# Token halves in block 1's feed-forward norm, and an early mean with squares per tile in block 2's norm

## The reference

```python
def first_block(...):                      # for l in range(2)
    ...
    x = x + g1 * (mix @ w_out[l])
    h = rmsnorm(x, norm_ffn_g[l]) * (1.0 + sc2) + sh2
    f = (silu(h @ ffn_w1[l]) * (h @ ffn_w3[l])) @ ffn_w2[l]
    x = x + g2 * f

def second_block(...):                     # for i in range(2)
    ...
    mix = concat([a_out, b_out]) @ w_o[i]
    x = layer_norm(ALPHA * x + mix, ln1_g[i], ln1_b[i])
    gate, up = split(x @ w_ffn_in[i], 2)
    ffn = (silu(gate) * up) @ w_ffn_out[i]
    ple = (p[i] @ w_ple[i]) * sigmoid(x @ w_ple_gate[i])
    x = layer_norm(ALPHA * x + ffn + ple, ln2_g[i], ln2_b[i])
```

## Time and profile before

| | before |
|---|---|
| median of 3 runs | 2498.53 us (2494.79 to 2498.84) |
| profiled execution | 2500.13 us |
| its span | 2498.3 us |
| mean granted clock of PE | 0.992 |
| busy: PE, DVE, ACT, POOL | 97%, 71%, 44%, 43% |

### The profile page before, as it was taken

The page is one execution under the profiler, slowest core; times in us unless marked ns, Lnnn a source line. Parts: engine busy times, 40 slices in busy tenths (PEclk is TensorE's granted clock), DMA queues, the critical chain, the costliest instruction groups (busy, mean ns, idle before and its releaser), DMA issues.

```text
span 2498.3 us, 35167 instructions
## 1 busy us (share of the span) xinstructions
PE 2424.8 (97%) x13615; PEld 2033.0 (81%) x13615; DVE 1765.1 (71%) x2671; ACT 1095.0 (44%) x1803; POOL 1065.5 (43%) x600
## 2 busy tenths in 40 slices
PE   6999999999999999999999999999999999999997
PEld 4777788988777788998777779999877777999985
...
DMA packets 239645, 268.87 MB, mean 108 GB/s; under 512 B 19976, under 2 KB 204024, under 8 KB 239224
## 3 DMA queue, kind: packets, MB, share of 16 engines
...
HBM read 264.51 MB, written 2.10 MB: 107 GB/s over the span
## 4 chain that ended last, share of the span: by engine, by line
PE 75%; DVE 10%; issue 5%; ACT 4%; POOL 3%; DMA 3%; SPq 1%; ACTq 0%; DVEq 0%; POOLq 0%
PE bank L2801 22%; PE bank L2803 22%; PE bank L2802 22%; DVE k_lo L2057 1%; DMA raw<-in_w_ffn_in 1%; DVE r L1908 1%; POOL w_lo L1652 1%; POOL k_lo L1663 1%; DMA raw<-in_ffn_w 1%; ACT k_hi L1105 1%; DVE u_sum L2074 1%; PE bank L3404 1%; PE bank L3470 1%; DVE u_t_raw L2087 1%; PE bank L3130 1%
## 5 line engine op out<-in xcount | busy, mean ns | idle before, releaser
L1663 POOL TENSOR_TENSOR k_lo<-raw,k_hi 128x512 fp32r<-128x512 f32 x297 | 430.0, 1459 | 542.9 <-ACT k_hi L1105 541.9
L1652 POOL TENSOR_TENSOR w_lo<-raw,w_hi 128x2048 fp32r<-128x2048 f32 x53 | 248.8, 4694 | 525.3 <-ACT w_hi L1051 446.3
L1105 ACT ACTIVATE k_hi<-raw 128x512 fp32r<-128x512 f32 x444 | 270.9, 626 | 310.7 <-PE bank L2803 249.4
L2801 PE MATMUL bank<-h_hi,k_lo 128*128 128x256 f32 (+1 forms) x1156 | 370.8, 321 | 3.8 <-DVE k_lo L2057 2.5
L2802 PE MATMUL bank<-h_lo,k_hi 128*128 128x256 f32 (+1 forms) x1156 | 369.6, 320 | 0.0
L2803 PE MATMUL bank<-h_hi,k_hi 128*128 128x256 f32 (+1 forms) x1156 | 369.5, 320 | 0.0
L2801 PE MATMUL bank<-h_hi,w_lo 128*128 128x512 f32 x800 | 325.0, 406 | 10.7 <-DVE h_lo L2017 3.9
L2803 PE MATMUL bank<-h_hi,w_hi 128*128 128x512 f32 x800 | 313.4, 392 | 0.0
L2802 PE MATMUL bank<-h_lo,w_hi 128*128 128x512 f32 x800 | 313.3, 392 | 0.0
L2801 PE MATMUL bank<-f_hi,k_lo 128*128 128x512 f32 x704 | 278.4, 395 | 8.6 <-DVE u_row L2118 2.9
L2801 PE MATMUL bank<-u_t_hi,k_lo 128*128 128x256 f32 x1008 | 282.6, 280 | 1.2 <-POOL k_lo L1663 1.2
...
## 6 DMA issues: line engine op xcount, KB each, us to landing
...
```

The source lines that it names most:

```text
L1105: act.activation(hi, src, ACT.Copy).then_inc(s.f_hi.up, 1)
L1652: pool.tensor_tensor(b.w_lo[p][:, 0:n], b.raw[p][:, 0:n], b.w_hi[p][:, 0:n].bitcast(F32), ALU.subtract)\
L1663: pool.tensor_tensor(lo, src, hi.bitcast(F32), ALU.subtract).then_inc(s.f_lo.up, 1)
L2801: pe.matmul(out, wlo, xhi, start=start, stop=False)
```

## The change

Block 1: the last tile of w_out is multiplied in two halves of 256 tokens, into two banks, behind `columns(1)`. Sum of squares, root, gain and shift and low part are done for the left 256 tokens and then for the right ones, with the sum for the left half inside the right half's products and that for the right half behind the first step of the feed-forward. `first_units` runs all eight channel tiles for the left half, then all for the right half, without dummies ahead of it; it counts `f_step` in the second half alone. The signals of the norm count halves, and SP waits for the right half's first low part before two loads of `b_raw`.

Block 2: while PE begins w_o, DVE sums the eight tiles of x as they are before w_o is added, PE makes the mean of this after the first k of `attended`, and DVE subtracts it. ACT squares each tile of x as w_o's tile is added (ahead of `split(15)`), PE sums four of the squares ahead of w_o's last tile and the others after it, with the mean of what the tiles now hold. The variance is the mean square less the square of this mean, and DVE subtracts the remaining mean tile by tile while it scales.

The core of the diff (the signals' counts, renamed signals and arguments that are only passed through are left out):

```diff
+HALVED = 1, 3
+LAST_BANK = 2, 1
...
-    sp.wait_ge(*s.hl(l * 2 + 1, 1))
+    sp.wait_ge(*s.hl(l * 2 + 1, KD + 1))
...
+def act_half_root(act, e, c, h):
+    s, b, bank, v = e.s, e.b, e.bank, HALVES[h]
+    act.wait_ge(*s.rms(c, 2 + h))
+    act.activation(b.r[:, v], bank[7][:, v], ACT.Ln, bias=b.eps[:, 0:1], scale=1.0 / D).then_inc(s.r.up, 1)
+    act.wait_ge(*s.r(c, 2 * h + 1))
+    act.activation(b.r[:, v], b.r[:, v], ACT.Exp, scale=-0.5).then_inc(s.r.up, 1)
+def act_half_scaled(act, e, c, h, gain, shift, full, ks):
+    s, b, v = e.s, e.b, HALVES[h]
+    for k in ks:
+        act.wait_ge(*s.xr(c, (KD + 1) * h + (k + 2 if k else 1)))
+        bias, scale = shift[:, k:k + 1], gain[:, k:k + 1]
+        act.activation(b.h_hi[:, k, v], b.sq[:, k, v], ACT.Identity, bias=bias, scale=scale).then_inc(s.hh.up, 1)
+        if k:
+            act.activation(full[:, k, v], b.sq[:, k, v], ACT.Identity, bias=bias, scale=scale).then_inc(s.hf.up, 1)
+def act_halves(act, e, c, gain, shift, full):
+    act_half_root(act, e, c, 0)
+    act_half_scaled(act, e, c, 0, gain, shift, full, range(0, 5))
+    act_half_root(act, e, c, 1)
+    act_half_scaled(act, e, c, 0, gain, shift, full, range(5, KD))
+    act_half_scaled(act, e, c, 1, gain, shift, full, range(KD))
...
         act_high(act, e, lay, q)
-    act_rms(act, e, l * 2 + 1, b.gain[:, 8:16], b.mod[:, 24:32], b.hf)
+    act_halves(act, e, l * 2 + 1, b.gain[:, 8:16], b.mod[:, 24:32], b.hf)
...
 def act_layer_norm(act, e, l):
     s, b, bank = e.s, e.b, e.bank
-    for k in range(KD):
-        act.wait_ge(*s.ld(l, k + 1))
-        act.activation(b.sq[:, k, :], b.x[:, k, :], ACT.Square).then_inc(s.lsq.up, 1)
     act.wait_ge(*s.lmean(l, 2))
-    act.activation(b.r[:, :], bank[7][:, :], ACT.Ln, bias=b.eps[:, 1:2], scale=1.0 / D).then_inc(s.l_r.up, 1)
-    act.wait_ge(*s.l_r(l, 1))
+    act.activation(b.sq[:, 1, :], bank[6][:, :], ACT.Square, scale=1.0 / D).then_inc(s.l_r.up, 1)
+    act.wait_ge(*s.var(l, 1))
+    act.activation(b.r[:, :], b.sq[:, 1, :], ACT.Ln, bias=b.eps[:, 1:2]).then_inc(s.l_r.up, 1)
+    act.wait_ge(*s.l_r(l, 2))
     act.activation(b.r[:, :], b.r[:, :], ACT.Exp, scale=-0.5).then_inc(s.l_r.up, 1)
     act_normed(act, e, l * 2, 0)
+def act_square_out(act, e, l, ks):
+    s, b = e.s, e.b
+    for k in ks:
+        act.wait_ge(*s.res(l, k + 1))
+        act.activation(b.sq[:, k, :], b.x[:, k, :], ACT.Square).then_inc(s.lsq.up, 1)
...
     split(14)
+    act_square_out(act, e, l, range(KD))
     split(15)
...
-    dve_square(dve, e, KD - 1, b.sq[:, KD - 1, :], lay.bank_out(1, Q_OUT + 1))
+    c, last = l * 2 + 1, KD - 1
     dve.wait_ge(*s.b_pe(l, 1))
     dve_gains(dve, e, l, 1)
+    def last_tile(h, signal):
+        v = HALVES[h]
+        dve.scalar_tensor_tensor(b.x[:, last, v], bank[LAST_BANK[h]][:, v], b.mod[:, 16 + last:17 + last],
+                                 b.x[:, last, v], ALU.mult, ALU.add).then_inc(signal.up, 1)
+    def last_square(h):
+        v = HALVES[h]
+        dve.tensor_tensor(b.sq[:, last, v], b.x[:, last, v], b.x[:, last, v], ALU.mult).then_inc(s.ssq.up, 1)
+    gain, shift = b.gain[:, 8:16], b.mod[:, 24:32]
+    dve.wait_ge(*s.rms(c, 1))
+    last_tile(0, s.ssq)
+    dve.wait_ge(*s.ssq(c, 7))
+    last_square(0)
+    dve.wait_ge(*s.tile(lay.pair(6), 1, 1))
+    last_tile(1, s.bank[1])
     dve.wait_ge(*s.gain(l, 2))
-    dve_rms(dve, e, l * 2 + 1, b.gain[:, 8:16], b.mod[:, 24:32], b.hf, s.hl)
+    dve_half_root(dve, e, c, 0, 0)
+    dve_half_full(dve, e, c, 0, gain, shift, b.hf)
+    dve_half_root(dve, e, c, 0, 1)
+    dve.wait_ge(*lay.bank_out(1, Q_OUT + 1))
+    last_square(1)
+    for k in range(2, KD):
+        dve_half_low(dve, e, c, 0, k - 2, b.hf, s.hl)
+        dve_half_root(dve, e, c, 0, k)
+    for k in (KD - 2, KD - 1):
+        dve_half_low(dve, e, c, 0, k, b.hf, s.hl)
+        dve_half_root(dve, e, c, 1, k - (KD - 2))
+        if k == KD - 2:
+            dve_half_full(dve, e, c, 1, gain, shift, b.hf)
+    for k in range(2, KD):
+        dve_half_low(dve, e, c, 1, k - 2, b.hf, s.hl)
+        dve_half_root(dve, e, c, 1, k)
+    for k in (KD - 2, KD - 1):
+        dve_half_low(dve, e, c, 1, k, b.hf, s.hl)
...
 def dve_layer_norm(dve, e, l):
     s, b, bank = e.s, e.b, e.bank
-    dve.wait_ge(*s.lmean(l, 1))
+    dve.wait_ge(*s.l_r(l, 1))
+    dve.wait_ge(*s.lmean(l, 3))
+    dve.scalar_tensor_tensor(b.sq[:, 1, :], bank[7][:, :], 1.0 / D, b.sq[:, 1, :], ALU.mult, ALU.subtract)\
+       .then_inc(s.var.up, 1)
+    for k in range(2):
+        dve_less_mean(dve, e, k, -1.0 / D)
+    dve.wait_ge(*s.l_r(l, 3))
     for k in range(KD):
-        dve.scalar_tensor_tensor(b.x[:, k, :], bank[6][:, :], -1.0 / D, b.x[:, k, :], ALU.mult, ALU.add)\
-           .then_inc(s.ld.up, 1)
-    dve.wait_ge(*s.l_r(l, 2))
-    for k in range(KD):
-        dve.wait_ge(*s.ld(l, k + 1))
+        dve.wait_ge(*s.ld(l, KD + k + 1))
         dve_scaled(dve, e, k)
         if k == 0:
             dve_normed(dve, e, l * 2, 0)
+        if k + 2 < KD:
+            dve_less_mean(dve, e, k + 2, -1.0 / D)
...
+def dve_early_shift(dve, e, lay, l):
+    s, b = e.s, e.b
+    for k in range(2):
+        dve.wait_ge(*lay.bank_out(k % 2, PART_USE[KD - 2 + k]))
+    dve.tensor_tensor(b.r[:, :], b.x[:, 0, :], b.x[:, 1, :], ALU.add).then_inc(s.lsum.up, 1)
+    for k in range(2, KD):
+        dve.wait_ge(*s.lsum(l, k - 1))
+        dve.tensor_tensor(b.r[:, :], b.r[:, :], b.x[:, k, :], ALU.add).then_inc(s.lsum.up, 1)
+    dve.wait_ge(*s.lmean(l, 1))
+    for k in range(KD):
+        dve_less_mean(dve, e, k, -1.0 / D)
...
+    dve_early_shift(dve, e, lay, l)
     for k in range(KD):
+        dve.wait_ge(*s.ld(l, k + 1))
         dve.wait_ge(*(s.att(l, 3 * (k // 4) + k % 4 + 1) if k % 4 < 3 else
                       s.tile(lay.pair(6), k // 4, 1)))
-        dve.wait_ge(*lay.bank_out(k % 2, PART_USE[k]))
         dve.tensor_tensor(b.x[:, k, :], b.x[:, k, :], bank[OUT2_BANK[k]][:, :], ALU.add).then_inc(s.res.up, 1)
...
+def pe_half_rms(pe, e, c, h, total, last):
+    s, v = e.s, HALVES[h]
+    pe.wait_ge(*s.ssq(c, 8 + h))
+    pe.matmul(e.bank[7][:, v], e.b.ones[:, :], total[:, v], start=True, stop=False)
+    pe.matmul(e.bank[7][:, v], e.b.ones[:, :], last[:, v], start=False, stop=True).then_inc(s.rms.up, 1)
+def pe_last_out(pe, e, lay, total):
+    s, b, c, j2, p = e.s, e.b, lay.l * 2 + 1, 6, 1
+    hi, lo = w8(b.w_hi[p]), w8(b.w_lo[p])
+    for h in range(2):
+        pe.wait_ge(*(lay.bank_free(1, Q_OUT + 1) if h else s.mo(lay.l, 1)))
+        v = HALVES[h]
+        for n, k in enumerate(MIX_ORDER):
+            if (h, n) == (1, 6):
+                pe_half_rms(pe, e, c, 0, total, b.sq[:, KD - 1, :])
+            op = three(pe, e.bank[LAST_BANK[h]][:, v], hi[:, k, P:2 * P], lo[:, k, P:2 * P], b.h_hi[:, k, v], b.h_lo[:, k, v],
+                       n == 0, n == KD - 1)
+        op.then_inc(s.half.up if h else s.rms.up, 1)
...
-        keep_busy(pe, e, bank[0])
-        for k in range(4):
-            for q in (k, 4 + k):
-                pe.wait_ge(*s.low_in(n, plan, q))
-            for c in range(2):
-                pe.wait_ge(*ready(2 * k + c))
-                for u in range(2):
-                    for m in range(2):
-                        op = plain(u, k, m, c, 2 * k + c, k == 0 and c == 0, k == 3 and c == 1)
-            op.then_inc(s.f_step.up, 1 if k < 3 else RING - 3)
+        for h in range(2):
+            for k in range(4):
+                if h == 0:
+                    for q in (k, 4 + k):
+                        pe.wait_ge(*s.low_in(n, plan, q))
+                for c in range(2):
+                    pe.wait_ge(*ready(h, 2 * k + c))
+                    for u in range(2):
+                        for m in range(2):
+                            op = plain(u, k, m, c, 2 * k + c, k == 0 and c == 0, k == 3 and c == 1, HALVES[h])
+                if h:
+                    op.then_inc(s.f_step.up, 1 if k < 3 else RING - 3)
+                elif k == 0:
+                    halfway(None, 0)
...
-    for j in range(2):
-        pe_unit(pe, e, lay, 12 + j, Q_OUT + j, order=MIX_ORDER)
+    pe_unit(pe, e, lay, 12, Q_OUT, order=MIX_ORDER)
+    pe_unit(pe, e, lay, 13, Q_OUT + 1, order=MIX_ORDER, ms=(0,))
     columns(1).then_inc(s.b_pe.up, 1)
-    pe_rms(pe, e, c + 1, b.sq[:, 0, :], b.sq[:, KD - 1, :])
-    pe_ffn(pe, e, lay, lambda k: s.hl(c + 1, k + 1), between)
+    pe_last_out(pe, e, lay, b.sq[:, 0, :])
+    def halfway(u, at):
+        pe_half_rms(pe, e, c + 1, 1, b.sq[:, 0, :], b.sq[:, KD - 1, :])
+    pe_ffn(pe, e, lay, lambda h, k: s.hl(c + 1, KD * h + k + 1), between, halfway)
...
 def pe_layer_norm(pe, e, l):
     s, b, bank = e.s, e.b, e.bank
-    pe.wait_ge(*s.lsum(l, 6))
+    pe_square_sums(pe, e, l, range(4, KD - 1))
+    pe.wait_ge(*s.lsum(l, 13))
+    pe.wait_ge(*s.ld(l, KD))
     pe.matmul(bank[6][:, :], b.ones[:, :], b.r[:, :], start=True, stop=False)
     pe.wait_ge(*s.res(l, KD))
```

(58 more changed lines are left out.)

40 lines of the change are left out of this document (22 added, 18 removed).

## The result

| | before | after |
|---|---|---|
| median | 2497.75 us (4 runs) | 2535.74 us (2531.98 to 2539.88, 4 runs) |
| profiled execution, its span | 2500.13, 2498.3 us | 2539.88, 2538.1 us |
| mean granted clock of PE | 0.992 | 0.983 |

The ratio is 1.0154, with a 95% interval of 1.0134 to 1.0175: 38 us slower, where 33.6 were forecast. In the profiled executions it is 39.75.

A forecast was written before the change was run, and what follows sets the result against it. TensorE, busy 97% of the span, was taken as the bound. Block 1's 5.2 and block 2's 11.6 us, over two layers, made 33.6 on 2500.13, 2533.7, less 1.6: 2532; range 2519 to 2542, with 0.8 between 2506 and 2542.

The forecast's parts named there:

- W_out's last tile, copies, root: Block 1, end of w_out: tile ends 1.9 us later, k_hi copies run 263.85 to 266.05, root there at 266.95.
- Restart of block 1: Block 1: VectorE's half operations wait for GpSimd's k_lo, first low part ends 271.4, TensorE restarts at 271.5: +1.0 us.
- The bound with nothing stalled: Block 1's restart if no VectorE operation waits for GpSimd: TensorE restarts at 268.85, -1.65 us.
- First units: Block 1's first units: 192 half-width matmuls plus the second half sum, 23.7 us for 21.90 (+1.8), plus 2 for half clock.
- rival E: Every extra matmul pays its weight load, 0.187 us, 240 of them, 45 us over the forecast: 2577 us, chance 0.02.
- The other side of block 1: Block 1, ScalarE's doubled scalings: 2.6 us more, TensorE's next unit +3.9 to +5.9; +5.2 a layer taken, bounds +2 and +6.5.
- rival C: Later waits in block 1's feed-forward swallow most of the 5.2 us, block 2 at its least +2.3: 2503 us, chance 0.08.
- SP's later b_raw loads: Block 1: two loads start some 10 us later, costed at nothing since their columns are wanted only after four feed-forward units.
- The early mean: Block 2, w_o: VectorE's seven adds, taking turns with GpSimd, stall TensorE 6.6 us a layer, plus 2 for the clock.
- Sums and restart of block 2: Block 2 after w_o: TensorE idles 3 us for GpSimd's w_lo before the dummies; first product +2.3 to +3.9, taken +3.
- Rival B: Block 2: adds are through before TensorE asks, no stall and no lost clock in w_o: 2517 us, chance 0.20.
- A: The forecast itself, 2532 us, chance 0.63; own range 2519 (block 1 at +2, block 2 at +9) to 2542.

The follow-up runs named there:

- the three edits: Changed kernel with 18 dummies ahead of block 1's first units, the second half's sum early and the left root ahead of ScalarE's k_hi copies: 2528.37 us, ratio 1.0123.

## Why the prediction was right

2535.74 lies in the range; the forecast of 2532 is 3.7 low. Block 2 came as worked out, and its room up to +15 a layer went unused; that kept the total in the range although block 1, 10.1 and 7.7 a layer, lies above its own bound of +6.5. So the nearness of the total is in part luck. Step by step:

- **W_out's last tile, copies, root: right.** Copies at 7.71 from the mark (forecast 7.65), root at 10.70 (10.75), POOL's k_lo at 8.41 (8.3).
- **Restart of block 1: right in kind, +0.45 for +1.0.** DVE's operations were held, two of them, not all. The half sum that comes early gives nothing, as forecast, but the run with the root ahead shows that ScalarE's queue, which the prediction blamed, isn't the only reason: GpSimd would have held VectorE anyway. (The bound with nothing stalled, 268.85, is 0.35 less than five operations of 0.45 from 266.95 give; the forecast doesn't use it.)
- **First units: right.** 26.1 us with the second sum and the half clock, 25.7 forecast. The 196 instructions in these 26.1 us, part of them at half clock, leave no room for a weight load paid by each: rival E is out. In the halved tile, whose matmuls each load 128 columns of weights, 39 matmuls start in 4.68 us, 0.12 each (the x41 counts two that began earlier), while the loads run beside them all that time. By the Trainium skill (TensorE: Matmul & The Clock Gate, "The mechanism") a load overlaps running matmuls only where their row groups differ; the trace doesn't agree with that sentence for this case, and the same section also lets a load into the background weight buffer go ahead.

```profile
256.34:261.02 4.68, 4.68 (x41) 4.68 (x40) 2.26 (x6) 0.48 (x1) 0.00 (x0) 1.00 0.00 0
```

- **The other side of block 1: mis-sized.** This is the step that failed: "ACT's 15 scalings of some 0.7 become 30 of 0.44, 2.6 more", and from it "+3.9 to +5.9". The next unit came 8.9 later. A half scaling has a pitch of 0.50 and not 0.44, so 30 take 14.9, where 15 whole ones take 10.6 (0.708 a step from 270.95 to 280.16 in the run with the whole norm): 4.3 more. And I missed that ScalarE's second root stands behind the scalings of the left half's first five tiles, and waits 2.83 for a sum that PE makes behind 24 matmuls, nearly all at half clock. The wait of 4.69 that this gives PE drew a second stretch of half clock. Making the norm whole again took 15.0 of 18.6 away, which shows that the halves of the norm, not the halved tile, are the cost. How the last scaling's 9.3 divide is read from ScalarE's rows: 4.3 for the operations, and 6.1 for gaps between the scalings (6.5 where they were 0.5: 2.2 behind the first scaling, for a DVE operation held beside GpSimd; 3.8 for the second sum and root; 0.6 for DVE), less 1.1 for the sooner start. Of this the three edits show 3.2.
- **Later waits took part of it back.** PE's 0.93 at 315.17 and, in the second layer, 2.36 at 960.01 of the kernel before have no counterpart after; the waits of 2.88 and 2.26 remained, at 3.10 and 2.27. So rival C's mechanism was there, at small size. SP's later b_raw loads, put at nothing, end no wait of PE over 0.25 us in the first layer.
- **The early mean: right.** 5.62 and 5.64 of wait for 6.6; the adds took the turns that were worked out, from 1425.54 to 1440.98 (15.4, forecast 16.0). Both runs on this term, POOL held back and the mean asked for later, behave by their marks as the mechanism says.
- **Sums and restart of block 2: right.** Idle 2.79 (forecast 3), dummies partly at half clock, and the whole block 11.7 and 11.3 for 11.6.
- **Rival B's size** is what the run with the later mean shows: 2520 without the stall, 2517 forecast.
- **A's lower end**, 2519, is 1.5 under what its two terms add up to, 2 x (2 + 9) on 2498.5; nothing hangs on it.
